# The low parts of a stage's weights: made by VectorE inside its attention steps, or by GpSimd beside them

## The chip, the cores and the metric

The kernel runs on one core of one Trainium2 chip. A core has TensorE (PE in the profile; the matrix products), VectorE (DVE), ScalarE (ACT), GpSimd (POOL) and SyncE (SP, which here only issues transfers). Each engine works through its own list of instructions in order; a wait on a semaphore holds up everything behind it on that engine. The time is device time in microseconds, from the first to the last work of the program.

## What is computed

Two transformer blocks over one sequence of 256 positions of width 2048. The first block, cut to what matters here:

```
proj = rms_norm(x, g_mix) @ w_in
q, k, v, x_gate, x_rec = split(proj)
y_attn = windowed_gqa_sink(rope(q), rope(k), v, sink)        # 16 query heads, 4 key heads
c = centred_depthwise_conv(x_rec)
h_rec = rg_lru(c, forward) + rg_lru(c, backward)             # two linear recurrences over time
y_lru = gelu(x_gate) * h_rec
x = x + concat(rms_norm(y_attn), rms_norm(y_lru)) @ w_out
x = x + peer(rms_norm(x), w_pq, keys, u_emb, v_emb)          # experts by product keys
```

The second block (a state space mixer, then dilated attention) follows and is not touched. All is computed in float32.

## The kernel before, in words

**Weights.** All weight matrices flow through one stream of tiles of 128 rows by 1024 columns, in the order of the list STREAM: "rec" 4 bodies, "q" 4, "kv" 2, "gate" 4, "w_out" 8, and so on; a body is four tiles. Each product in float32 is made of three products of TensorE, with weights and activations each split in a high and a low part: w_hi x_hi, w_hi x_lo, w_lo x_hi. A tile therefore goes through four hands, in four buffers u = 0 to 3: SyncE loads it into `raw[u]` (it waits until the low part of the tile four before is made, semaphore lo_done); ScalarE rounds it to `w_hi[u]` (`high`, L1281; waits for the load and for TensorE to have used the tile four before; semaphore hi_done); VectorE or GpSimd subtracts, w_lo = raw - w_hi (`low`, L1797 on VectorE, L475 on GpSimd; semaphore lo_done); TensorE uses it (semaphore tile_used). Since lo_done counts tiles in order, exactly one engine makes the low parts at any time. VectorE does in most stages; GpSimd in the stages that call `lows` ("gate", the first 12 bodies of "up0", and "xbc").

**The stage of the change** is "gate": the 16 tiles of x_gate's weights, one in each of 16 steps s. All engines run a loop over s written out in the same order, and in it lie the attention of the first block and the recurrences. The attention goes in 8 rounds n (row half tt and key head g). With SCORES_AT = (3, 5, 7, 9, 10, 12, 13, 14) as the steps of the rounds' scores, a round is:
- TensorE: `scores(n)` (L739) in step SCORES_AT[n]; `turn_probs(n)` (L750) two steps after that entry; `values(n)` (L762) one step later still. In a step it does first the gate tile (`gate_half`, 24 products of L564 to L566), then values, then turning, then scores.
- VectorE: `maxima(n)` in step SCORES_AT[n]: scale and mask the scores (L2013), maximum (L2016), three small operations on 128x4 (L2017, L2018, L2019); before the first of them it waits for the probabilities of the round before, which read the same buffer. `head_rows(n)` in the step of the values: two small operations (L2025, L2026) and the scaling of the values (L2029).
- ScalarE: at the head of step s, `high` for tile s + 4; in odd steps the copy of a finished gate block (L1411); then `turned_probs` (L1429), then `probs(n)` (L1418, L1420), in step SCORES_AT[n] or, for rounds 4, 6 and 7, one step later.
- VectorE besides: scan(0) in step 2, drive(1) in step 4, scan(1) in step 6, the sum of both directions in step 8 (`gate_work`, L2036).

The low part that belongs to step s is, as the high part, that of tile s + 4: in steps 0 to 11 tiles 4 to 15 of "gate", in steps 12 to 15 tiles 0 to 3 of "w_out". Tiles 0 to 3 of "gate" are VectorE's from the stage before ("kv"). Before the change GpSimd makes these sixteen, each when its high part is there. It first waits for rope_done, which VectorE signals when the keys are rotated.

After step 15 TensorE has fillers (`spare_products`) between values(6), turn_probs(7) and values(7); then the attention's rows are turned (L813) and the products of "w_out" begin.

Of the kernel before, what the change touches and what calls it, by code (L numbers as in the profile page):

```python
# [91 lines left out]
FIRST_BODY = {}  # L92
# [57 lines left out]
def build(nc, a, out):  # L150
    ctx = ExitStack()
    with ctx:
# [8 lines left out]
        def sem(name):  # L161
            if name not in names:
                names[name] = ctx.enter_context(nc.semaphore(name))
            return names[name]
# [296 lines left out]
        def _(pool):  # L461
# [10 lines left out]
            def low(body, u):  # L472

                pool.wait_ge(hi_done, 4 * body + u + 1)
                pool.tensor_tensor(w_lo[:, u, :], raw[:, u, :], w_hi[:, u, :].bitcast(F32), ALU.subtract)\  # L475
                    .then_inc(lo_done, 1)

            def lows(name, start=0, end=None):
                if start == 0:
                    pool.wait_ge(lo_done, 4 * (FIRST_BODY[name] + 1))  # L480
                with pool.Fori(start, end or NB[name]) as j:
                    for u in range(4):
                        low(j + (FIRST_BODY[name] + 1), u)
# [3 lines left out]
                pool.dma_start(decay_rows[:, n % 4, :], decay_kept[n].partition_broadcast(P))\  # L487
                    .then_inc(sem(f"decay_loaded{n % 4}"), 16)

            pool.wait_ge(sem("rope_done"), 1)  # L490
            lows("gate")
            pool.wait_ge(sem("x1_done"), 1)
            pool.dma_start(skT, a["skT"]).then_inc(sem("keys_loaded"), 16)
            lows("up0", 0, POOL_BODIES)
# [1296 lines left out]
        def _(dve):  # L1791
            link = Chain(dve, dve_link)

            def low(body, u):

                dve.wait_ge(hi_done, 4 * body + u + 1)
                dve.tensor_tensor(w_lo[:, u, :], raw[:, u, :], w_hi[:, u, :].bitcast(F32), ALU.subtract)\  # L1797
                    .then_inc(lo_done, 1)
# [164 lines left out]
            def drive(dr):  # L1963

                x = ii[:, dr, :, :]
                dve.wait_ge(sem("root_done"), dr + 1)
                link(dve.scalar_tensor_tensor(wide(x), wide(x), 0.5, wide(rr[:, dr, :, :]), ALU.mult, ALU.mult))

            def scan(dr):

                a0, u0, o0 = wide(aa[:, dr, :, :]), wide(ii[:, dr, :, :]), wide(rr[:, dr, :, :])
                if dr:
                    a0, u0, o0 = a0[:, ::-1], u0[:, ::-1], o0[:, ::-1]
                link(dve.tensor_tensor_scan(o0, a0, u0, 0.0, ALU.mult, ALU.add))
# [32 lines left out]
            def maxima(n):  # L2007
                tt, g = steps[n]
                dve.wait_ge(sem("scores_done"), n + 1)
                if n:  # L2010
                    dve.wait_ge(sem("probs_done"), n)
                window = cw[:, CW["window"] + tt * S:CW["window"] + (tt + 1) * S].unsqueeze(1).to_broadcast([P, 4, S])
                dve.scalar_tensor_tensor(sc[:, :, :], banks(0, 2).rearrange("p (h s) -> p h s", s=S),  # L2013
                                         HD ** -0.5, window, ALU.mult, ALU.add).then_inc(sem("scores_read"), 1)
                dve.wait_ge(sem("scores_read"), n + 1)
                link(dve.tensor_reduce(sm[:, n, 0, :], sc[:, :, :], AX.X, ALU.max))  # L2016
                link(dve.tensor_tensor(sm[:, n, 0, :], sm[:, n, 0, :], sinkb[:, 4 * g:4 * g + 4], ALU.max))  # L2017
                link(dve.tensor_tensor(sm[:, n, 1, :], sinkb[:, 4 * g:4 * g + 4], sm[:, n, 0, :], ALU.subtract))  # L2018
                dve.tensor_scalar(sm[:, n, 0, :], sm[:, n, 0, :], -1.0, None, ALU.mult).then_inc(sem("max_done"), 1)  # L2019

            def head_rows(n):

                tt, g = steps[n]
                dve.wait_ge(sem("probs_done"), n + 1)
                link(dve.tensor_tensor(sm[:, n, 1, :], sm[:, n, 1, :], sm[:, n, 2, :], ALU.add))  # L2025
                link(dve.reciprocal(sm[:, n, 1, :], sm[:, n, 1, :]))  # L2026
                dve.wait_ge(sem("pv_done"), n + 1)
                o = yn[:, tt, g * S:(g + 1) * S].rearrange("p (i r d) -> p r i d", i=2, r=2)
                dve.tensor_tensor(o, PS[:, 6, 0:S].rearrange("p (r i d) -> p r i d", r=2, i=2),  # L2029
                                  sm[:, n, 1, :].rearrange("p (r i) -> p r i", r=2).unsqueeze(3)  # L2030
                                  .to_broadcast([P, 2, 2, HD]), ALU.mult).then_inc(sem("attn_out"), 1)
# [3 lines left out]

            gate_work = {2: lambda: scan(0), 4: lambda: drive(1), 6: lambda: scan(1), 8: both_directions}  # L2036
            for s in range(16):
                if s in VALUES_AT:
                    head_rows(VALUES_AT.index(s))
                if s in SCORES_AT:  # L2040
                    maxima(SCORES_AT.index(s))
                if s in gate_work:
                    gate_work[s]()
# [906 lines left out]
```

## Time and profile before

| | us |
|---|---|
| median of 3 runs | 3260.49 (3260.39 to 3261.94) |
| the profiled execution, its own time | 3260.77 |
| its span, first to last instruction | 3259.1 |
| TensorE busy | 3208.9 (98%) |
| VectorE busy | 2372.4 (73%) |
| ScalarE busy | 1578.0 (48%) |
| GpSimd busy | 650.9 (20%) |

The mean granted clock of TensorE is 0.994 of full speed. The 1.7 us between the span and the execution's own time lie around the recorded instructions. Busy times of TensorE are those of overlapping products, so idle time shows where it waited, but a busy engine need not be at its peak. In timelines a row is one instruction or several alike in sequence (x and their number); a bracket tells how long the engine was idle before it and what ended that.

### The profile page before, as it was taken

Reading aid. Unit: us, or ns where it says so; the run is one execution under the profiler, and the core shown is the slowest. Engines: PE = TensorE matmul, PEld = TensorE weight load, DVE = VectorE, ACT = ScalarE, POOL = GpSimd, SP = SyncE. Lnnn points to the kernel's source line nnn. Section 1 sums busy time; section 2 is a strip of 40 time slices with the busy share of each in tenths; the row PEclk is TensorE's granted clock in tenths of the full one; section 3 lists DMA queues with packets and bytes.
Section 4 is the critical chain, followed back from the end, with each engine's and each line's share of the span. In section 5 each row is a group of like instructions: output and inputs, shape, how many; then the busy total and the mean of one; then the engine's idle time right before and its main releaser. Section 6 shows DMA issues by size and latency. Waiting matters only on the chain.

```text
span 3259.1 us, 64800 instructions
## 1 busy us (share of the span) xinstructions
PE 3208.9 (98%) x22152; PEld 2946.2 (90%) x22152; DVE 2372.4 (73%) x3842; ACT 1578.0 (48%) x2226; POOL 650.9 (20%) x635
## 2 busy tenths in 40 slices
PE   9999999999999999999999999999999999999997
PEld 8888999999889998899878889999998879988996
DVE  6665468499778997799999775434898877555556
ACT  4755444433454344433444556545766444344443
POOL 1050038200111001100000115886221111100000
PEclk9999999999999999999999999999999999999999
DMA  6435556666787678866655884666776877766444
GB/s 214 146 104 163 173 164 182 190 214 214 247 264 224 214 221 260 264 202 210 202 177 180 263 262 144 185 188 197 241 235 193 290 263 233 247 200 187 149 136 155
DMA packets 185940, 667.86 MB, mean 205 GB/s; under 512 B 24193, under 2 KB 24417, under 8 KB 184529
## 3 DMA queue, kind: packets, MB, share of 16 engines
q1 hardware_dynamic: 149984, 545.91, 54.0%
q0 software_dynamic: 35824, 120.19, 11.9%
q8 instruction: 84, 1.38, 0.2%
q14 instruction: 48, 0.39, 0.0%
HBM read 663.83 MB, written 2.18 MB: 204 GB/s over the span
## 4 chain that ended last, share of the span: by engine, by line
PE 91%; DVE 5%; ACT 2%; issue 1%; DMA 0%; DVEq 0%; ACTq 0%; SPq 0%
PE PS L564 16%; PE PS L566 16%; PE PS L565 16%; PE PS L924 7%; PE PS L928 7%; PE PS L926 7%; PE PS L642 2%; PE PS L641 2%; PE PS L643 2%; PE PS L1106 2%; PE PS L1108 2%; PE PS L1110 2%; PE PS L879 1%; DVE w_lo L1797 1%; PE PS L801 1%
## 5 line engine op out<-in xcount | busy, mean ns | idle before, releaser
L1281 ACT ACTIVATE w_hi<-raw 128x1024 fp32r<-128x1024 f32 x1032 | 1093.0, 1060 | 1500.8 <-PE PS L566 847.0
L1797 DVE TENSOR_TENSOR w_lo<-raw,w_hi 128x1024 fp32r<-128x1024 f32 x872 | 1065.5, 1224 | 563.1 <-ACT w_hi L1281 556.9
L564 PE MATMUL PS<-xt_hi,w_hi 128*128 128x256 f32 x4608 | 1324.8, 287 | 6.0 <-DVEq L1929 2.1
L565 PE MATMUL PS<-xt_lo,w_hi 128*128 128x256 f32 x4608 | 1305.8, 283 | 0.0
L566 PE MATMUL PS<-xt_hi,w_lo 128*128 128x256 f32 x4608 | 1305.4, 283 | 0.0
L564 PEld LDWEIGHTS PS<-xt_hi,w_hi 128*128 128x128 f32 x4608 | 885.7, 192 | 15.9 <-issue 12.9
L565 PEld LDWEIGHTS PS<-xt_lo,w_hi 128*128 128x128 f32 x4608 | 886.3, 192 | 0.4
L566 PEld LDWEIGHTS PS<-xt_hi,w_lo 128*128 128x128 f32 x4608 | 885.8, 192 | 0.0
L475 POOL TENSOR_TENSOR w_lo<-raw,w_hi 128x1024 fp32r<-128x1024 f32 x160 | 393.3, 2470 | 361.2 <-ACT w_hi L1281 234.9
L924 PE MATMUL PS<-w_hi,st_hi 128*128 128x512 f32 x1024 | 401.9, 393 | 0.3
L928 PE MATMUL PS<-w_lo,st_hi 128*128 128x512 f32 x1024 | 398.8, 389 | 0.0
L926 PE MATMUL PS<-w_hi,st_lo 128*128 128x512 f32 x1024 | 398.7, 389 | 0.0
L499 POOL DMA_DIRECT2D ada<-in_ada_w x240 | 129.2, 538 | 1226.6 <-DVE acc_down L2214 632.6
L928 PEld LDWEIGHTS PS<-w_lo,st_hi 128*128 128x128 f32 x1024 | 192.2, 188 | 40.4
L924 PEld LDWEIGHTS PS<-w_hi,st_hi 128*128 128x128 f32 x1024 | 192.2, 188 | 40.1 <-ACT hid L1536 1.6
L926 PEld LDWEIGHTS PS<-w_hi,st_lo 128*128 128x128 f32 x1024 | 192.3, 188 | 38.9
L641 PE MATMUL PS<-w_hi,xt_hi 128*128 128x512 f32 x352 | 141.4, 402 | 0.0
L642 PE MATMUL PS<-w_hi,xt_lo 128*128 128x512 f32 x352 | 138.6, 394 | 0.0
L643 PE MATMUL PS<-w_lo,xt_hi 128*128 128x512 f32 x352 | 138.4, 393 | 0.0
L1899 DVE TENSOR_SCALAR cbuf<-PS,pc 128x256 f32<-128x256 f32 x48 | 23.2, 484 | 152.0 <-PE PS L566 130.3
L2205 DVE TENSOR_REDUCE gate_sum<-PS 128x256 f32<-128x768 f32 x128 | 121.8, 951 | 0.0
L2185 DVE TENSOR_TENSOR hot<-iota,slotsT 128x256 bf16<-128x256 bf16 (+1 forms) x256 | 113.6, 485 | 0.5 <-DVE slot_gate L2171 0.5
(404 smaller groups left out, 3483.8 us busy)
## 6 DMA issues: line engine op xcount, KB each, us to landing
raw<-in_u_emb SPq DMA_DIRECT2D x256, 512.0 KB, 3.8
raw<-in_v_emb SPq DMA_DIRECT2D x256, 512.0 KB, 4.5
ada<-in_ada_w POOLq DMA_DIRECT2D x240, 256.0 KB, 4.5
raw<-in_xbc SPq DMA_DIRECT2D x96, 512.0 KB, 3.7
raw<-in_z SPq DMA_DIRECT2D x80, 512.0 KB, 3.7
raw<-in_q SPq DMA_DIRECT2D x64, 512.0 KB, 3.6
raw<-in_a_out SPq DMA_DIRECT2D x64, 512.0 KB, 4.5
raw<-in_k SPq DMA_DIRECT2D x48, 512.0 KB, 4.4
```

The source lines that it names most:

```text
L475: pool.tensor_tensor(w_lo[:, u, :], raw[:, u, :], w_hi[:, u, :].bitcast(F32), ALU.subtract)\
L564: pe.matmul(o, w_h, x_h, start=start, stop=False, skip_group_check=True)
L565: pe.matmul(o, w_h, x_l, start=False, stop=False, skip_group_check=True)
L566: return pe.matmul(o, w_l, x_h, start=False, stop=stop, skip_group_check=True)
L641: pe.matmul(o, source[0][:, k, t], w_hi[:, u, c:c + 512], start=k == 0, stop=False)
L642: pe.matmul(o, source[1][:, k, t], w_hi[:, u, c:c + 512], start=False, stop=False)
L643: last = pe.matmul(o, source[0][:, k, t], w_lo[:, u, c:c + 512], start=False, stop=k == KC - 1)
L924: pe.matmul(o, st(st_hi, st2_hi, u)[:, t], w_hi[:, u, c], start=start, stop=False, skip_group_check=True)
L926: pe.matmul(o, st(st_lo, st2_lo, u)[:, t], w_hi[:, u, c], start=False, stop=False, skip_group_check=True)
L928: last = pe.matmul(o, st(st_hi, st2_hi, u)[:, t], w_lo[:, u, c], start=False, stop=stop, skip_group_check=True)
L1281: act.activation(w_hi[:, u, :], raw[:, u, :], ACT.Copy).then_inc(hi_done, 1)
L1797: dve.tensor_tensor(w_lo[:, u, :], raw[:, u, :], w_hi[:, u, :].bitcast(F32), ALU.subtract)\
```

## The change

The two lines by which GpSimd waits for rope_done and makes the low parts of the "gate" stage are taken out. In VectorE's loop over the 16 steps a call of `low` stands first in each step, ahead of head_rows, maxima and the recurrences' work; it makes the low part of tile s % 4 of body FIRST_BODY["gate"] + 1 + s // 4, thus of tile s + 4. It waits for hi_done of that tile.

```diff
--- before.py
+++ after.py
@@ -487,8 +487,6 @@
                 pool.dma_start(decay_rows[:, n % 4, :], decay_kept[n].partition_broadcast(P))\
                     .then_inc(sem(f"decay_loaded{n % 4}"), 16)
 
-            pool.wait_ge(sem("rope_done"), 1)
-            lows("gate")
             pool.wait_ge(sem("x1_done"), 1)
             pool.dma_start(skT, a["skT"]).then_inc(sem("keys_loaded"), 16)
             lows("up0", 0, POOL_BODIES)
@@ -2035,6 +2033,7 @@
 
             gate_work = {2: lambda: scan(0), 4: lambda: drive(1), 6: lambda: scan(1), 8: both_directions}
             for s in range(16):
+                low(FIRST_BODY["gate"] + 1 + s // 4, s % 4)
                 if s in VALUES_AT:
                     head_rows(VALUES_AT.index(s))
                 if s in SCORES_AT:
```

`low` on VectorE, unchanged (L1794 to L1798):

```python
def low(body, u):

    dve.wait_ge(hi_done, 4 * body + u + 1)
    dve.tensor_tensor(w_lo[:, u, :], raw[:, u, :], w_hi[:, u, :].bitcast(F32), ALU.subtract)\
        .then_inc(lo_done, 1)
```

## Rows read from the trace of the kernel before

**Rows 1.** The page, part 1: engine, busy us (share of the span), instructions.

```profile
PE 3208.9 (98%) x22152; PEld 2946.2 (90%) x22152; DVE 2372.4 (73%) x3842; ACT 1578.0 (48%) x2226; POOL 650.9 (20%) x635
```

**Rows 2.** Windows: stretch, length, then PE, PEld, DVE, ACT, POOL busy, clock, DMA, GB/s.

```profile
158.00:241.00 83.00, 76.91 (x622) 71.51 (x621) 55.27 (x70) 47.14 (x108) 47.53 (x16) 0.98 0.37 109
...
167.50:176.50 9.00, 3.47 (x28) 3.07 (x27) 8.71 (x6) 2.31 (x10) 6.43 (x3) 1.00 0.54 148
...
176.50:184.00 7.50, 7.50 (x50) 6.53 (x50) 3.18 (x7) 4.37 (x10) 4.70 (x2) 0.77 0.46 115
```

**Rows 3.** Timeline of PE, 160 to 238 us: start, length, instruction, [idle before, releaser].

```profile
160.43 0.36 PE L564 MATMUL PS<-xt_hi,w_hi 128*128 128x256 f32 x1
...
163.56 1.13 PE L739 MATMUL PS<-kT,qT 64*128 64x256 f32 x8
...
169.31 0.39 PE L564 MATMUL PS<-xt_hi,w_hi 128*128 128x256 f32 x1 [1.56 <-POOL w_lo L475]
...
176.42 1.09 PE L750 MATMUL PS<-cc,pr 128*128 128x128 f32 x8 [3.97 <-ACT pr L1420]
...
177.44 1.92 PE L739 MATMUL PS<-kT,qT 64*128 64x256 f32 x8
...
197.37 1.04 PE L750 MATMUL PS<-cc,pr 128*128 128x128 f32 x8
...
234.65 1.97 PE L762 MATMUL PS<-kvn,pT 128*128 128x64 f32 x16 [0.38 <-DVE qn L2029]
```

**Rows 4.** Timeline of DVE, 150 to 235 us, same columns.

```profile
150.76 2.36 DVE L1797 TENSOR_TENSOR w_lo<-raw,w_hi 128x1024 fp32r<-128x1024 f32 x2
...
158.27 2.29 DVE L1967 SCALAR_TENSOR_TENSOR ii<-ii,rr 128x2048 f32<-128x2048 f32 x1
...
160.59 6.51 DVE L1974 TENSOR_TENSOR_SCAN rr<-aa,ii 128x2048 f32<-128x2048 f32 x1
...
179.45 1.22 DVE L2013 SCALAR_TENSOR_TENSOR sc<-PS,cw 128x1024 f32<-128x1024 f32 x1 [3.10 <-PE PS L739]
...
182.44 0.16 DVE L2025 TENSOR_TENSOR sm<-sm 128x4 f32<-128x4 f32 x1
...
185.38 4.42 DVE L1974 TENSOR_TENSOR_SCAN rr<-aa,ii 128x2048 f32<-128x2048 f32 x1
...
189.91 1.23 DVE L2013 SCALAR_TENSOR_TENSOR sc<-PS,cw 128x1024 f32<-128x1024 f32 x1
...
228.97 1.23 DVE L2013 SCALAR_TENSOR_TENSOR sc<-PS,cw 128x1024 f32<-128x1024 f32 x1 [3.97 <-ACT pr L1420]
...
233.67 0.15 DVE L2025 TENSOR_TENSOR sm<-sm 128x4 f32<-128x4 f32 x1
...
234.42 0.15 DVE L2025 TENSOR_TENSOR sm<-sm 128x4 f32<-128x4 f32 x1
```

**Rows 5.** Timeline of ACT, 163 to 227 us.

```profile
163.64 1.06 ACT L1281 ACTIVATE w_hi<-raw 128x1024 fp32r<-128x1024 f32 x1
...
182.56 0.20 ACT L1418 ACTIVATE sm<-sm 128x4 f32<-128x4 f32 x1 [3.13 <-DVE sm L2019]
...
184.64 1.04 ACT L1281 ACTIVATE w_hi<-raw 128x1024 fp32r<-128x1024 f32 x1
...
226.70 0.20 ACT L1418 ACTIVATE sm<-sm 128x4 f32<-128x4 f32 x1
```

**Rows 6.** Timeline of POOL, 177 to 195 us.

```profile
177.39 4.70 POOL L475 TENSOR_TENSOR w_lo<-raw,w_hi 128x1024 fp32r<-128x1024 f32 x2 [3.46 <-ACT w_hi L1281]
...
185.76 8.55 POOL L475 TENSOR_TENSOR w_lo<-raw,w_hi 128x1024 fp32r<-128x1024 f32 x2 [3.67 <-ACT w_hi L1281]
```

**Rows 7.** Groups of instructions by line, 155 to 235 us: busy, mean ns | idle before.

```profile
L2017 DVE TENSOR_TENSOR sm<-sm,sinkb 128x4 f32<-128x4 f32 x8 | 7.9, 993 | 0.3
...
L2018 DVE TENSOR_TENSOR sm<-sinkb,sm 128x4 f32<-128x4 f32 x8 | 3.4, 428 | 0.3
```

## The prediction

> **What bounds the kernel now.** The page's busy times come first [rows 1]: TensorE (PE) is busy for 3208.9 of 3259.1 us and VectorE (DVE) for 2372.4, so over the whole kernel any idle time of PE goes into the total and VectorE has room. The reader should not stop there, for the change touches one stage, from about 158 to 241 us. Cut into windows [rows 2], that stage has PE busy for 76.91 of 83 us, VectorE for 55.27, ScalarE (ACT) for 47.14, GpSimd (POOL) for 47.53. So PE idles 6.1 us there, and most of it is in one stretch: 3.47 busy of 9.00 us from 167.5 on, followed by 7.5 us at a granted clock of 0.77. PE's timeline [rows 3] names the waits: 1.56 us at 169.31 for a low part from GpSimd, 3.97 us at 176.42 for the first attention probabilities (ACT), 0.38 at 234.65. Then come 8 score products in 1.92 us, where the same 8 take 1.13 at 163.56: the slow clock, met after the idle, costs 0.8 us there and about as much in the gate tile behind it.
>
> VectorE's timeline [rows 4] and ScalarE's [rows 5] show the attention going round: scores (PE), maxima (DVE), probabilities (ACT), turning and values (PE). Every round also contains work of each engine's own order. Today the low parts are outside that ring: GpSimd makes each as soon as ScalarE has the high part [rows 6], and nothing of the attention stands behind it. It isn't free: the small VectorE operation L2017 takes 0.99 us in the mean and L2018 0.43, where L2025, of their size, takes 0.15 at 233.67 [rows 4, 7], and the first scan 6.51 instead of 4.42 [rows 4]. That is 8 x 0.84 + 8 x 0.27 + 2.09 = 10.9 us of VectorE time held up by GpSimd. L2013, which reads one operand from PSUM, is not held: 1.23 us at 189.91, while GpSimd is at work (8.55 us from 185.76), as against 1.22 at 179.45 [rows 4, 6].
>
> The Trainium skill (GPSIMD Engine Reference, Key points) says that GpSimd shares its SBUF interfaces with VectorE, with contention for instructions that have two SBUF inputs. The trace agrees in its sizes (0.99 us against 0.15 for L2017, nothing for L2013), and by that rule the 10.9 us come back; it says nothing on where in VectorE's order the new work stands.
>
> **Part by part.**
>
> *Removed from GpSimd:* 16 subtractions, its wait for the turned keys, and its two loop waits. Its next work waits for x1_done, long after the stage, so nothing there starts sooner. No DMA is issued by the moved steps; the raw loads are released by the same count (SP waits for lo_done), each by a later low part. A low part comes at most about 8 us later than now, but the raw tile it releases is wanted only four tiles further on; I cost that at nothing, with 1 us as upper bound if a load were late.
>
> *Added to VectorE:* 16 subtractions; two in a row take 2.36 us, so 1.18 each [rows 4], 18.9 us. Minus the 10.9 us given back that is 8.0 us more in 83, of which VectorE idles 27.7 [rows 2]. By sums it fits.
>
> *Added wait:* this is what decides. The low part at the head of step s is that of tile s+4, and VectorE waits in order for its high part. ScalarE makes that one at the head of its own step s, and in its order it stands behind the probabilities of the round before. Behind VectorE's waiting instruction stand head_rows, the scans, and the next maxima. So a round that was maxima, probabilities (then VectorE free) becomes maxima, probabilities, high part, low part, head_rows, extras, next maxima, one after the other.
>
> Terms, from rows: maxima start to ScalarE's exponential 182.56-179.45 = 3.11; probabilities to the next high part 184.64-182.56 = 2.08; high part start to the dependent low part 185.76-184.64 = 1.12 (GpSimd's wait; I take VectorE's as the same); low part 1.18; head_rows 234.42-233.67 = 0.75; scan 189.91-185.38 = 4.53; drive and the sum of directions 2.29 each (158.27) [rows 4 to 6]. From a maxima's start M to the next low part's start is 3.11+2.08+1.12 = 6.31.
>
> *The first round gains.* Drive starts at 158.27 and ends at 160.56; the lows of tiles 4, 5, 6 follow at once (their high parts are done; the last of tile 7 is begun at 163.64 [rows 5]) until 164.10; the scan without GpSimd until 168.63; low of tile 7, and M0 = 169.81. The probabilities are out at M0+3.11+2.08 = 175.0, where PE now waits until 176.42: 1.3 to 1.4 us sooner, and the wait at 169.31 is gone within it.
>
> *The later rounds lose.* Each M is the last plus 6.31 plus what step order puts behind the wait:
> M1 = 169.81 + 6.31 + low, drive, low (1.18+2.29+1.18) = 180.77.
> M2 = + 6.31 + low, head_rows, scan, low (7.64) = 194.72; today 189.91 [rows 4].
> M3 = + 6.31 + low, head_rows, sum, low (5.40) = 206.43.
> M4, M5 = + 6.31 + low, head_rows (1.93) = 214.67, 222.91.
> M6 = the same, 231.15.
> M7 waits only for the probabilities before it (it reuses their buffer): 3.11 + (228.97-226.70 = 2.27) = 236.53; today 228.97.
> Then maxima 2.99 (182.44-179.45), the low part of step 15 1.18, head_rows to PE 234.65-233.67 = 0.98: the seventh values product (index 6) starts at 241.68 instead of 234.65, 7.0 us late [rows 3 to 5].
>
> Is anything else later than that? PE's own work up to there would be done at about 241.4: the scores of the last round wait for the masking of M6, 1.26 us after it (the pitch of L2013) = 232.4, then 1.1 of scores, 3.1 of gate tile (160.43 to 163.56), 1.8 of values, 0.9 of turning (both by their pitch), and 16 spare products at 3.13/24 = 0.13 each, 2.1 [rows 3]. So up to 0.3 us of PE slack, and none to spare for a slower clock. Behind it stand the last turning, the second filler, and the last values, whose chain through ScalarE keeps pace (its probabilities done at about 241.8, PE turns from 243.5). From there to the output projection the work is one chain, and behind that PE is saturated, so the delay stays.
>
> *The clock.* New idle times of PE: before it turns probabilities 2, which come 0.15 after M2+5.19, at 200.1 (today 197.37 [rows 3]; PE, 1.3 us ahead, is there at about 196.2, so 3.9 us idle), and before probabilities 4 at M4+5.3 = 220.0, where it is at about 217.3 (2.7 us idle). The idle of 3.97 us now is followed by the slow clock [rows 2, 3]; I expect this after the first of them and perhaps after the second, 1.6 us of PE each time. Both lie where PE waits again for VectorE within the round (for the masking of M3 and of M6, some 0.8 and 1.4 us by the same reckoning), so I take 0 and keep 1.5 as the upper end. The bounds of the whole stage: if VectorE's waits cost nothing, all of PE's present losses there, 1.56+3.97+0.38 and 1.6 of clock, = 7.5 us, would be gained; if none of the terms overlaps and the clock adds twice, 7.0+3.2 = 10.2 lost.
>
> **Sum.** +7.0 us against the profiled execution (3260.77 us, span 3259.1) gives 3267.8; the median of the three runs is 0.28 lower, so 3267.5.
>
> **Rivals.**
>
> *Hidden.* Same time: VectorE has 27.7 idle us in the stage and needs 8.0 more; PE works 77 of 83 us and could cover the shifts. For it: the low part of a tile is needed four tiles later, and the first probabilities come earlier. Against it: the maxima, not the low parts, are what becomes late, and PE has just 6 us of slack in the stage. It would give -1.4 (the first round's gain kept) to +4, say 3261.5.
>
> *Faster: the held operations were the price.* Where VectorE's attention operations lie on PE's waits, the 10.9 us held up by GpSimd were paid by PE; the 3.97 us wait at 176.42 stands behind the first scan and maxima, both held. If ScalarE's high parts are ready whenever VectorE comes for them, the low costs 1.18 and saves more. It decides if the later high parts start before the probabilities of their round; the code's order says they don't from step 4 on. The bound is -7.5, so 3253.0.
> The Trainium skill (GPSIMD Engine Reference, Performance versus the Vector engine) gives elementwise work to VectorE as a rule, GpSimd being about 2x slower; the trace has 2.35 against 1.18 us per low part [rows 4, 6], and by that rule the time falls as here.
>
> *Slower by more.* The ring as forecast, and the slow clock after two new idles not absorbed, or high parts late also from PE: +8.7 to +10.2, say 3270.
>
> **Chances.** The ring 0.75, with its own range 3265.5 to 3269.2; slower by more 0.10; hidden 0.11; faster 0.04. A change of 0.2% is 6.5 us, about what a measurement of this kernel tells from none, so 3267.0 is the edge, and the forecast lies only 0.5 above it. Of the ring's 0.75 I put 0.48 above the edge, as the clock can only add. Slower 0.10+0.48 = 0.58; same 0.27+0.11 = 0.38; faster 0.04. The range leaves out the fast rival and part of the extremes: 3263.3 to 3270.3.
>
> **What the new profile would show.** No GpSimd subtraction between 158 and 241 us, and 16 more on VectorE. L2017 near 0.16 us in every round and both scans near 4.42. The first turning of probabilities near 175, the third at about 200 instead of 197.4, the seventh values at 241.7. VectorE waiting for ScalarE's high part, 6.31-2.99 = 3.3 us in each of steps 4, 6, 8, 10 and 13, 2.1 in step 12. PE idle about 3.9 us before the third turning. I am wrong if VectorE's waits at the low parts are short, if the maxima start no later than now in rounds 2 to 7, or if the seventh values come within 4 us of today's 234.65. If they come 7 us late but the total is less, something downstream gave it back.

## The result

| | before | changed |
|---|---|---|
| median of 14 runs, us | 3260.35 (3255.24 to 3263.71) | 3267.76 (3265.46 to 3270.60) |
| ratio to before | | 1.0021, 95% interval 1.0014 to 1.0028 |
| the profiled execution: own time / span | 3260.77 / 3259.1 | 3269.16 / 3267.5 |
| VectorE busy / GpSimd busy, us | 2372.4 / 650.9 | 2378.7 / 602.8 |

The change costs 7.4 us by the medians (6.8 by the ratio), by the interval 0.14% to 0.28%. VectorE is busy for only 6.3 us more although it makes sixteen subtractions of 1.18 us more, 18.9 us: most of what they take was taken before by GpSimd's hold, that is by the time that VectorE's small operations and scans lasted longer while GpSimd subtracted.

### The profile page after: what moved, and what is told of

Its sections match the earlier page's. It is cut to its first block, busy times and chain, and to the rows that moved or that the text cites. A ratio compares the mean times of both kernels' runs of the same rounds, so it can differ in the third digit from the quotient of the medians.

```text
span 3267.5 us, 64794 instructions
## 1 busy us (share of the span) xinstructions
PE 3211.3 (98%) x22152; PEld 2947.5 (90%) x22152; DVE 2378.7 (73%) x3858; ACT 1577.5 (48%) x2226; POOL 602.8 (18%) x619
## 3 DMA queue, kind: packets, MB, share of 16 engines
q8 instruction: 84, 1.38, 0.2%
## 4 chain that ended last, share of the span: by engine, by line
PE 89%; DVE 6%; ACT 3%; issue 2%; DMA 0%; DVEq 0%; ACTq 0%; SPq 0%
PE PS L562 16%; PE PS L564 16%; PE PS L563 16%; PE PS L922 7%; PE PS L926 7%; PE PS L924 7%; PE PS L639 2%; PE PS L641 2%; PE PS L640 2%; PE PS L1104 2%; PE PS L1108 2%; PE PS L1106 2%; PE PS L877 1%; DVE w_lo L1795 1%; PE PS L803 1%
## 5 line engine op out<-in xcount | busy, mean ns | idle before, releaser
L1795 DVE TENSOR_TENSOR w_lo<-raw,w_hi 128x1024 fp32r<-128x1024 f32 x888 | 1084.7, 1223 | 586.6 <-ACT w_hi L1279 581.2
L475 POOL TENSOR_TENSOR w_lo<-raw,w_hi 128x1024 fp32r<-128x1024 f32 x144 | 345.7, 2412 | 203.8 <-ACT w_hi L1279 203.8
```

## The profile after

Line numbers of the changed kernel are 2 lower than those of before up to VectorE's loop (maxima's L2013 is L2011, the two small operations L2017 and L2018 are L2015 and L2016, `low` is L1795), as two lines of GpSimd's are gone; in the experiments' kernels the same instruction can again stand up to three lines off. To compare executions I count from the start of drive(0), the last thing that VectorE does before the sixteen steps, to the turning of the attention's rows on PE (L811, L813 before), which ends the stage. That stretch in the kernel before and in the changed one (columns as in [rows 2]):

```profile
158.27:243.49 85.22, 78.93 (x638) 73.33 (x635) 55.79 (x73) 48.47 (x111) 47.53 (x16) 0.98 0.36 106
```

```profile
159.78:252.88 93.10, 83.22 (x638) 76.72 (x635) 63.48 (x89) 48.33 (x111) 0.00 (x0) 0.93 0.32 97
```

The stretch went from 85.22 to 93.10 us, 7.88 us more. PE did the same 638 products; it idled 9.9 us instead of 6.3, and was busy for 4.3 us more, which is clock: 0.93 granted instead of 0.98. Those 4.3 us are not what the clock costs: PE would in part have waited in their place, as the run fill shows below. GpSimd does nothing there.

The change begins 1.5 us later in this execution (159.78 instead of 158.27), which is not the change's. Two microseconds near each kernel's start show why, first the kernel before, then the changed one (columns as in [rows 2]):

```profile
47.00:49.00 2.00, 2.00 (x19) 2.00 (x18) 1.93 (x3) 0.00 (x0) 0.00 (x0) 1.00 0.34 90
```

```profile
47.00:49.00 2.00, 2.00 (x12) 2.00 (x11) 1.95 (x3) 0.00 (x0) 0.00 (x0) 0.50 0.50 117
```

At the same point, after the same idle of 2.11 us, the clock fell in one execution (0.50) and not in the other (1.00). Of all ten kernels profiled for this study, four start the stage at 159.8 to 159.9 and six at 158.2 to 158.5. So 8.4 us of span is 1.5 of that, 7.9 of the stage, and 1.0 given back later (from 260 us up to 3240, the changed kernel has five windows of 20 us with the clock below 0.995, the kernel before seven). The stage alone is the fair measure of one profiled execution, and I use it below beside the timed medians.

VectorE's timeline in the changed kernel answers [rows 4]:

```profile
159.78 2.29 DVE L1965 SCALAR_TENSOR_TENSOR ii<-ii,rr 128x2048 f32<-128x2048 f32 x1
162.10 3.50 DVE L1795 TENSOR_TENSOR w_lo<-raw,w_hi 128x1024 fp32r<-128x1024 f32 x3
165.51 4.42 DVE L1972 TENSOR_TENSOR_SCAN rr<-aa,ii 128x2048 f32<-128x2048 f32 x1
...
171.11 1.22 DVE L2011 SCALAR_TENSOR_TENSOR sc<-PS,cw 128x1024 f32<-128x1024 f32 x1
...
173.61 0.16 DVE L2015 TENSOR_TENSOR sm<-sm,sinkb 128x4 f32<-128x4 f32 x1
...
177.36 1.22 DVE L1795 TENSOR_TENSOR w_lo<-raw,w_hi 128x1024 fp32r<-128x1024 f32 x1 [3.18 <-ACT w_hi L1279]
...
181.97 1.22 DVE L2011 SCALAR_TENSOR_TENSOR sc<-PS,cw 128x1024 f32<-128x1024 f32 x1
...
188.22 1.23 DVE L1795 TENSOR_TENSOR w_lo<-raw,w_hi 128x1024 fp32r<-128x1024 f32 x1 [3.19 <-ACT w_hi L1279]
...
195.70 1.22 DVE L2011 SCALAR_TENSOR_TENSOR sc<-PS,cw 128x1024 f32<-128x1024 f32 x1
...
207.29 1.22 DVE L2011 SCALAR_TENSOR_TENSOR sc<-PS,cw 128x1024 f32<-128x1024 f32 x1
...
215.44 1.21 DVE L2011 SCALAR_TENSOR_TENSOR sc<-PS,cw 128x1024 f32<-128x1024 f32 x1
...
224.79 1.22 DVE L2011 SCALAR_TENSOR_TENSOR sc<-PS,cw 128x1024 f32<-128x1024 f32 x1 [1.13 <-PE PS L737]
...
232.93 1.21 DVE L2011 SCALAR_TENSOR_TENSOR sc<-PS,cw 128x1024 f32<-128x1024 f32 x1
...
238.95 1.23 DVE L2011 SCALAR_TENSOR_TENSOR sc<-PS,cw 128x1024 f32<-128x1024 f32 x1 [1.82 <-ACT pr L1418]
```

The reader should see three things. The scan takes 4.42 us and L2015 0.16 (6.51 and up to 2 us before): the hold is gone. The bracket of 3.18 us at 177.36 is VectorE idle at the low part of tile 8, with maxima's successor done and nothing allowed past it. And maxima (L2011) start 11.33, 22.19, 35.92, 47.51, 55.66, 65.01, 73.15 and 79.17 us after the drive. ScalarE's side of one round:

```profile
185.06 0.21 ACT L1416 ACTIVATE sm<-sm 128x4 f32<-128x4 f32 x1 [5.60 <-DVE sm L2017]
...
187.15 1.04 ACT L1279 ACTIVATE w_hi<-raw 128x1024 fp32r<-128x1024 f32 x1
```

From maxima 181.97 to the exponentials 185.06 is 3.09, to the high part 187.15 another 2.09, to the low part 188.22 another 1.07: 6.25 us where I reckoned 6.31, and 6.25 or 6.26 in each of the rounds 0 to 5. All of VectorE's waits, in one row (engine and line, released by: us, times, longest):

```profile
DVE w_lo L1795 <- ACT w_hi L1279: 18.0, 6, 3.2
```

PE's timeline answers [rows 3]:

```profile
176.43 1.97 PE L748 MATMUL PS<-cc,pr 128*128 128x128 f32 x8 [4.28 <-ACT pr L1418]
178.33 2.08 PE L737 MATMUL PS<-kT,qT 64*128 64x256 f32 x8
...
201.02 1.09 PE L748 MATMUL PS<-cc,pr 128*128 128x128 f32 x8 [2.19 <-ACT pr L1418]
...
208.56 0.70 PE L737 MATMUL PS<-kT,qT 64*128 64x256 f32 x4 [0.59 <-DVE sc L2011]
...
220.76 1.97 PE L748 MATMUL PS<-cc,pr 128*128 128x128 f32 x8 [2.44 <-ACT pr L1418]
222.66 2.08 PE L737 MATMUL PS<-kT,qT 64*128 64x256 f32 x8
...
244.09 1.92 PE L760 MATMUL PS<-kvn,pT 128*128 128x64 f32 x16
```

PE waits for probabilities 0, 2 and 4, and once for the masking of round 3. After the first and the third of these waits turning and scores take 1.97 and 2.08 us instead of 1.09 and 1.13. The seventh values, at 244.09, have no bracket: PE came to them without waiting.

## The experiments

Each was timed in the same rounds as the kernel before, in three groups: the changed kernel (before: 3260.35), the next four (3261.32), the last four (3260.74). Kernels of different groups are compared by their ratios to before. The intervals are those of this ratio; the stage is that of each one's profiled execution.

| kernel | low parts by | where in VectorE's step | median, us | ratio (95%) | stage, us |
|---|---|---|---|---|---|
| before | GpSimd | - | 3260.35 to 3261.32 | 1 | 85.2 |
| changed | VectorE | first | 3267.76 | 1.0021 (1.0014 to 1.0028) | 93.1 |
| low_last | VectorE | last | 3256.35 | 0.9986 (0.9977 to 0.9995) | 82.0 |
| wait_only | GpSimd | a wait first | 3269.24 | 1.0025 (1.0016 to 1.0035) | 95.9 |
| high_first | VectorE | first | 3262.18 | 1.0001 (0.9992 to 1.0011) | 84.9 |
| fill | VectorE | first | 3268.09 | 1.0022 (1.0013 to 1.0031) | 92.0 |
| head_wait_low_last | VectorE | a wait first, the work last | 3261.72 | 1.0002 (0.9992 to 1.0011) | 84.6 |
| low_last_fill | VectorE | last | 3256.85 | 0.9987 (0.9978 to 0.9996) | 80.4 |
| scan_later | VectorE | last, scans later | 3253.37 | 0.9979 (0.9969 to 0.9988) | 77.1 |
| before_scan_later | GpSimd | -, scans later | 3258.35 | 0.9991 (0.9982 to 1.0000) | 82.7 |

**low_last: the same work, another place.** Against the changed kernel:

```diff
             for s in range(16):
-                low(FIRST_BODY["gate"] + 1 + s // 4, s % 4)
                 ...
                 if s in gate_work:
                     gate_work[s]()
+                low(FIRST_BODY["gate"] + 1 + s // 4, s % 4)
```

> The same sixteen subtractions on VectorE as in the changed kernel, but last in each step, behind maxima and the recurrences' work. Theory (the place in VectorE's order is the price): the first maxima starts about 168.6 + what the stage starts late, no maxima after it waits for a high part, so the ring of 6.3 us is gone and the subtractions lie in VectorE's idle time: faster than before by 2.4 (first probabilities earlier) to 4.5 us (no slow clock in addition), about 3257. Rival (the work itself, 19 us more on VectorE, is the price): as the changed kernel, 3267. Rival (GpSimd's hold on VectorE mattered by itself): -5 to -7, about 3254.

Measured 3256.35, and 0.9986 of before. VectorE's timeline of it:

```profile
168.65 1.22 DVE L2011 SCALAR_TENSOR_TENSOR sc<-PS,cw 128x1024 f32<-128x1024 f32 x1
...
175.08 1.23 DVE L1795 TENSOR_TENSOR w_lo<-raw,w_hi 128x1024 fp32r<-128x1024 f32 x1
177.35 1.22 DVE L2011 SCALAR_TENSOR_TENSOR sc<-PS,cw 128x1024 f32<-128x1024 f32 x1 [1.05 <-PE PS L737]
```

The second maxima starts 8.70 us after the first, not 10.86, and its bracket names PE's scores: VectorE waits for the attention, no longer for a high part. No low part of the stage waits. The work of sixteen subtractions is there in full, so the work is not the price, its place is. The rival that it is the work falls. The timed interval (1.6 to 7.5 us of gain) doesn't part the theory's 2.4 to 4.5 from the third case's 5 to 7; the stage, 3.2 us shorter than before, speaks for the theory, which had 2.4 to 4.5.

**wait_only: the wait without the work.** Against the kernel before:

```diff
             for s in range(16):
+                dve.wait_ge(hi_done, 4 * (FIRST_BODY["gate"] + 1) + s + 1)
```

> The kernel before (GpSimd makes the low parts) with one wait at the head of each of VectorE's 16 steps, for the high part of tile s + 4, and no work added. Theory: the wait alone closes the ring; without the 1.18 us of each low part, but with GpSimd's hold, the maxima of rounds 2 to 6 are late by 1 to 3 us and the seventh values start 2 to 3.5 us late: about 3263, a bit less than half of the change's loss. Rival (the work is the price): no change, 3260.4. Rival (the wait is all of it): +7, 3267.

Measured 3269.24, ratio 1.0025: as much lost as by the change, and I had expected less than half. The forecast of this run missed. By the count alone the rival "the wait is all of it" wins. The trace says otherwise. VectorE and then GpSimd:

```profile
189.42 0.17 DVE L2025 TENSOR_TENSOR sm<-sm 128x4 f32<-128x4 f32 x1 [3.20 <-ACT w_hi L1281]
...
190.18 5.93 DVE L1974 TENSOR_TENSOR_SCAN rr<-aa,ii 128x2048 f32<-128x2048 f32 x1
```

```profile
189.47 8.84 POOL L475 TENSOR_TENSOR w_lo<-raw,w_hi 128x1024 fp32r<-128x1024 f32 x2 [3.66 <-ACT w_hi L1281]
```

Both engines were released by the same high part. GpSimd's two subtractions, 4.7 us when undisturbed [rows 6], run at the same time as the scan, which takes 5.93 us instead of 4.42. All six of these waits of VectorE end within 0.06 us of GpSimd's, and behind the wait everything is on the ring. VectorE's sum of directions takes 3.80 us there instead of 2.28, and a small operation 2.38:

```profile
221.74 2.38 DVE L2025 TENSOR_TENSOR sm<-sm 128x4 f32<-128x4 f32 x1 [3.25 <-ACT w_hi L1281]
```

That the hold (1.4 to 2.2 us behind each of the six waits) took the place of the low part's 1.18 us is my reading of these rows; this run by itself cannot part wait and work, and the next one does.

**head_wait_low_last: the wait without work and without hold.** Against low_last:

```diff
             for s in range(16):
+                dve.wait_ge(hi_done, 4 * (FIRST_BODY["gate"] + 1) + s + 1)
```

> low_last (subtractions last in each step) with the wait for the high part of tile s + 4 put back at the head of each step, and no work there. It parts the wait from the 1.18 us of subtraction behind it, without GpSimd's hold, which wait_only had in the ring as well. Stage lengths, from the start of drive(0) to the turning of the rows: before 85.2, changed kernel 93.1, low_last 82.0, wait_only 95.9. Theory (each round of the ring is 3.11 + 2.08 + 1.12 = 6.31 us and then everything that stands behind the wait, so the wait decides only where 6.31 plus that is above what PE needs for a round): M1 at 20.0 after the drive's start, M2 32.7, M3 43.2, M4 50.3, M5 57.3, M6 64.4, M7 69.8, stage 83.7 to 84.5, time 1.5 to 2.5 us above low_last: about 3258.5. Rival (the wait itself is the whole price): stage 92 to 93, time 3267.

```profile
174.91 2.29 DVE L1965 SCALAR_TENSOR_TENSOR ii<-ii,rr 128x2048 f32<-128x2048 f32 x1 [2.06 <-ACT w_hi L1279]
...
184.65 0.17 DVE L2023 TENSOR_TENSOR sm<-sm 128x4 f32<-128x4 f32 x1 [2.07 <-ACT w_hi L1279]
```

```profile
158.46:243.09 84.63, 78.90 (x638) 73.40 (x635) 63.47 (x89) 48.40 (x111) 0.00 (x0) 0.98 0.35 107
```

The maxima came at 19.92, 32.53, 43.00, 50.01, 57.55, 64.57 and 70.69 us after the drive, each within 0.9 us of the reckoning, and the stage at 84.63, just above the 83.7 to 84.5 forecast and 2.6 above low_last. The time missed its forecast: the ratio is 0.0016 above low_last's, 5 us where 1.5 to 2.5 were expected, with intervals that leave room for 2.6 as well as for more. So the wait alone costs 2.6 us of stage, and the low part at the head the other 8.5 of the 11.1 us between low_last and the changed kernel. The changed kernel's maxima are later than these by 1.14, 2.27, 3.39, 4.51, 5.65, 7.46, 8.58 and 8.48 us: one low part more (1.12 to 1.14) ahead of each of the maxima 0 to 6, and ahead of the sixth maxima (round 5) another 0.7, where VectorE waits for the scores that the slow clock delayed.

**high_first: the ring opened at ScalarE.** Against the changed kernel, on ScalarE:

```diff
 def gate_half(s):
     ...
-    high(FIRST_BODY["gate"] + s // 4 + 1, s % 4)
+    if s - 1 not in PROBS_AT[:6]:
+        high(FIRST_BODY["gate"] + s // 4 + 1, s % 4)
 ...
     if s in PROBS_AT:
+        if s in PROBS_AT[:6]:
+            high(FIRST_BODY["gate"] + (s + 1) // 4 + 1, (s + 1) % 4)
         probs(PROBS_AT.index(s))
```

> The changed kernel, but ScalarE makes the high part of step s + 1 ahead of the probabilities of rounds 0 to 5 in step s, not behind them. VectorE's low parts stay at the head of its steps. Theory (the ring closes over ScalarE's order): VectorE then waits at the low parts for under 1 us each instead of 3.2, the maxima come with the scores again, and the time is below that of before by 1 to 3 us, about 3258.5. Rival (the low parts' own 1.18 us ahead of the maxima are the price, whatever ScalarE does): 3264 to 3267. Rival (the probabilities, now behind a high part, become late): above 3262 with PE waiting for them.

Measured 3262.18: by the ratios 0.0020 of the 0.0021 are back with VectorE's order untouched, but not the gain over before that I had put on it (1 to 3 us). VectorE's waits at the low parts came down from 18.0 us to 7.0 in all, not to under 1 us each: the longest is 2.5. PE and ScalarE show the rest of the miss:

```profile
215.45 1.09 PE L748 MATMUL PS<-cc,pr 128*128 128x128 f32 x8 [1.54 <-ACT pr L1419]
```

```profile
212.28 1.06 ACT L1279 ACTIVATE w_hi<-raw 128x1024 fp32r<-128x1024 f32 x1 [1.49 <-PE PS L564]
213.24 0.19 ACT L1417 ACTIVATE sm<-sm 128x4 f32<-128x4 f32 x1
```

ScalarE waited 1.49 us for PE to be done with tile 12 before it could make the high part, and the probabilities of round 4 stood behind that; PE then waited 1.54 us for them. The ring was cut, and a shorter one made: the third rival, and PE waited by it in one round of six. Taken with the last run, the stage is 82.0 us with neither, 84.6 with the wait at the head and no work there, 84.9 with the work at the head and shorter waits, and 93.1 with both in full: the two together cost more than their sum, since then the work stands in the ring in every round. (The comparison is a rough one, as high_first also moves ScalarE's high parts.)

**fill: the clock in the changed kernel.** On PE:

```diff
                 if s in VALUES_AT:
                     values(VALUES_AT.index(s))
+                if s in (5, 12):
+                    spare_products(28 if s == 5 else 16, 7)
```

> The changed kernel, with products of no use (28 ahead of the first turning of probabilities, 16 ahead of the turning in step 12) in two idle stretches of PE of 4.3 and 2.4 us. If the slow clock behind the second idle is what made PE itself late at the end (scores and gate tile 13 took about 3 us more there, of which 0.9 us was left at the seventh values): granted clock 1.0 through the stage, VectorE no longer waits 1.1 us for the scores of round 5, and 0.9 us less than the changed kernel: about 3266.5. If the ring alone sets the time: the clock is back but the time is that of the changed kernel, 3267.5. If the fillers run into the wanted products: above 3268.

```profile
221.00:230.00 9.00, 9.00 (x74) 8.02 (x73) 5.00 (x10) 4.41 (x12) 0.00 (x0) 1.00 0.22 66
```

```profile
222.73 1.23 DVE L2013 SCALAR_TENSOR_TENSOR sc<-PS,cw 128x1024 f32<-128x1024 f32 x1 [0.61 <-PE PS L737]
...
241.35 1.97 PE L760 MATMUL PS<-kvn,pT 128*128 128x64 f32 x16 [0.21 <-DVE qn L2029]
```

The same stretch of the changed kernel, 221 to 230 us, had a clock of 0.66. Here it is 1.00, VectorE's wait for the scores of round 5 is 0.61 instead of 1.13, and the seventh values stand 83.14 us after the drive with a wait for VectorE in front, where the changed kernel has 84.31 without. The ring by itself thus gives 83.1 (I had reckoned 83.4), and the clock added 1.2. The clock was not full through the whole stage, as I had expected; the mean is 0.96. With the first idle filled PE is earlier and idles longer ahead of the third turning, and the clock falls there:

```profile
199.47 1.97 PE L748 MATMUL PS<-cc,pr 128*128 128x128 f32 x8 [3.86 <-ACT pr L1420]
```

That costs nothing, for the maxima of round 3 start 47.54 us after the drive, in the changed kernel 47.51. The timed median shows no gain: 3268.09, where 3266.5 was expected and 3267.5 if the ring alone sets the time. So the 1.2 us rest on the two profiled executions.

**low_last_fill** has 20 such products (of no use to the result) in step 5 of low_last, where PE idled 3.15 us.

> low_last with 20 products of no use ahead of the first turning of probabilities, where PE idled 3.15 us and the granted clock fell after it. If the clock is what that idle costs in addition: granted clock 1.0 through the stage, stage 80.4 instead of 82.0, time 1.0 to 1.6 us below low_last, about 3255. Rival (in the rounds behind, PE waits for maxima anyway): stage 81.5 to 82, no change.

```profile
158.26:238.70 80.44, 79.33 (x657) 74.54 (x655) 63.27 (x89) 48.45 (x111) 0.00 (x0) 1.00 0.36 112
```

In the profiled execution it is as the theory has it, 80.44 instead of 82.00 at a clock of 1.00. Timed it is no different from low_last (0.9987 and 0.9986; 3256.85, where about 3255 was expected). Whether the 1.6 us arrive at the end stays open.

**scan_later: what was late to begin with.** Against low_last:

```diff
-gate_work = {2: lambda: scan(0), 4: lambda: drive(1), 6: lambda: scan(1), 8: both_directions}
+gate_work = {4: lambda: drive(1), 6: lambda: scan(0), 8: lambda: scan(1), 11: both_directions}
```

> low_last with scan(0) in step 6 instead of 2, scan(1) in 8 instead of 6 and the sum of directions in 11 instead of 8, so that the first maxima has no scan ahead of it. Theory: M0 at 6.4 after the drive's start (10.2 in low_last), first turning at 12.3 without idle of PE, no slow clock, no maxima late by over 2 us after it; stage 77.2, time about 3251.6, 0.27% below before. Rival (the scans, now between later rounds, make those late): M3 or M2 several us after its scores, PE waiting for probabilities 2 or 3, stage 79 to 82, 3253 to 3256.

```profile
166.41 1.23 DVE L2011 SCALAR_TENSOR_TENSOR sc<-PS,cw 128x1024 f32<-128x1024 f32 x1 [0.67 <-PE PS L737]
```

```profile
159.92:237.00 77.08, 76.71 (x638) 72.12 (x635) 63.27 (x89) 48.46 (x111) 0.00 (x0) 1.00 0.37 117
```

The first maxima waits for the scores (0.67 us) and is not behind a scan, PE is busy 76.71 of 77.08 us, and the clock is full. 3253.37 against 3260.74 in the same rounds: 7.4 us below before and, by the ratios, some 14 below the changed kernel. Of all kernels here this is the fastest; its gain is clear of noise (0.9979, up to 0.9988). The stage is the theory's (77.2); the time, forecast at 3251.6, came out in the rival's 3253 to 3256, though PE shows no wait above 0.3 us in the stage, which was the rival's cause.

**before_scan_later** has the same table of scans in the kernel before, with GpSimd's low parts.

> The kernel before (GpSimd makes the low parts) with the same later places of the scans and the sum. If the late first maxima is its main loss: M0 at 6.5, first turning at about 13.8, stage 79.8 to 81, time 4 to 5.5 us below before: about 3256. Against scan_later it shows what GpSimd's hold on VectorE costs when nothing else is late: 2 to 3.5 us. Rival (the hold falls on the scans and the small operations and eats the gain): stage 83 to 85, 3258 to 3261.

```profile
158.51:241.25 82.74, 78.87 (x637) 73.43 (x635) 56.28 (x73) 48.65 (x111) 43.45 (x16) 0.98 0.37 109
```

```profile
L2017 DVE TENSOR_TENSOR sm<-sm,sinkb 128x4 f32<-128x4 f32 x8 | 8.3, 1041 | 0.3
L2018 DVE TENSOR_TENSOR sm<-sinkb,sm 128x4 f32<-128x4 f32 x8 | 5.6, 701 | 0.3
```

The gain is small, 2.4 us by the medians and with an interval that reaches 1.0000: the stage lies between theory and rival, the time in the rival's range. With the scans out of the way GpSimd's hold falls on the two small operations inside maxima: 8 x 0.88 and 8 x 0.54 us = 11.4 us. Against scan_later only the maker and place of the low parts differ: 82.74 against 77.08 us of stage, 3258.35 against 3253.37. Taking the low parts from GpSimd is thus worth 4 (by the ratios) to 5.7 us (by the stages) where the place is right, more than the 2 to 3.5 expected. How much of it is the hold and how much the slower subtraction (2.35 against 1.18 us) is not parted; PE has no wait for a low part in either stage.

## Why the prediction was right

3267.5 was forecast, 3267.76 measured, and the stage by itself lost 7.9 us where 7.0 were reckoned. By its steps:

- *First round gains.* M0 was to come 11.54 after the drive and came 11.33; the first turning was to be 1.3 to 1.4 us sooner and is 1.5 (16.65 us after the drive, 18.15 before). Right.
- *Later rounds lose.* The reckoned maxima, counted from the drive: 22.50, 36.45, 48.16, 56.40, 64.64, 72.88, 78.26. Measured: 22.19, 35.92, 47.51, 55.66, 65.01, 73.15, 79.17. The first five are early by 0.1 to 0.2 us a round, of which 0.06 is that VectorE is released 1.07 and not 1.12 us after the high part's start. The last three are late by the clock (below); in fill they came at 64.52, 72.67 and 78.04. low_last, high_first and head_wait_low_last show each link of the ring as a cause.
- *VectorE's added work.* 18.9 us less 10.9 of hold given back, 8.0, were reckoned; in the stage VectorE is busy for 63.48 instead of 55.79 us, 7.7 more.
- *VectorE's waits.* 3.3 us in five steps and 2.1 in one were forecast; the trace has 3.2 and 2.1, 18.0 in all.
- *The clock at nothing.* This term was mis-sized. I had the slow clock after the first new idle and its loss absorbed. It came after the idle ahead of round 4, where the slack was not enough: VectorE waited 1.13 us for the scores of round 5, and PE came to the seventh values 0.9 us later than the ring as reckoned. The profiled execution of fill puts 1.2 us on it, inside the 1.5 I had kept as an upper end; the timed medians don't show it.
- *PE's new idle before the third turning.* Forecast 3.9, measured 2.19. The slow clock after the first idle (4.28 us) lasted through turning, scores and half a gate tile, so PE was itself late at that point; with that idle filled (fill) the third was 3.86. The time of the turning, 41.2 us after the drive against 41.8 reckoned, was right because VectorE set it.
- *The delay stays.* It did, to about 1 us: 7.9 in the stage, and 6.9 of it at the end of that execution once the 1.5 from before the stage are taken off.
- *The low part's load at nothing.* No wait for a load appears in the stage that was not there before.

The rival "hidden" had the right sums (8 us of work for 27 idle) and fell because those idle microseconds lie behind waits. The fast rival had a part that is real: with the low parts last in the step, having them made by VectorE is worth 4 to 5.7 us. It fell by its own condition, that the high parts be ready. That the total came within 0.3 us is in part luck: neither the clock's 1.2 us nor the later 1.0 given back is in the sum, and the two nearly cancel.

## What to carry to other kernels

What work costs on an engine that has room depends on what stands behind it in that engine's order, and not on its duration alone (the same subtractions: a stage of 93.1 us first in the step, 82.0 last). So put a waiting instruction at the point of a step where its input is already there and nothing urgent follows. Before a wait is placed, write down the ring it closes (who releases it, and what that engine has in front of it), sum one round, and compare it with the round of the bounding engine. A change may be right in who does the work and wrong in where: the same sixteen subtractions cost 7.4 us first in the step, and last in it they gain 4.6 us (0.0014 of the time).

## What the runs showed of the hardware

- GpSimd and VectorE hold each other. With two SBUF operands on VectorE and a subtraction of GpSimd's begun before, an operation of 0.16 us took up to 2.4, the sum of directions 3.80 us instead of 2.28, a scan 5.93 or 6.51 instead of 4.42. Where VectorE's operation began first, GpSimd's took longer: in wait_only L1967, begun at 178.93, took its usual 2.29 us, and the subtraction begun at 178.98 took 4.49 instead of 2.35. Operations with an operand in PSUM (L2013, 1.22 us) or a single one (L2016, 1.22) were not touched.
- Two engines released by one semaphore met in all six rounds of wait_only (0.02 to 0.06 us apart); its stage is 95.9 us, and that of the same wait with the subtractions made by VectorE 84.6.
- PE's granted clock went from 1.00 to 0.50 after idles of 2.4 to 4.3 us in these stages, but the length of the idle alone doesn't tell: after 1.54, 1.56, 1.71 and 2.19 us it did not fall, after the idle of 2.11 us near 46 us it fell in four executions of ten, and in before_scan_later it fell after 1.38:

```profile
209.86 1.97 PE L750 MATMUL PS<-cc,pr 128*128 128x128 f32 x8 [1.38 <-ACT pr L1420]
```

- Products that nobody needs kept it full at 221 to 230 us (1.00 instead of 0.66).
